# Token loads, side stores, the last chunk and the first gather moved in a one-core hybrid decoder step

## What is computed

```
mod = silu(c) @ w_ada + b_ada                     # six vectors of 1024 for each of 9 sequences
h   = rmsnorm(x, g_pre_mix) * (1 + sc_mix) + sh_mix
u, qkv, z, a, b = split(h @ w_in)
pool_out = pool_mixer(u)                          # windows of 2, 4, 8, 16
q, k, v  = silu(causal_conv(qkv)); g, beta from a, b
o = gated_delta_rule(l2norm(q), l2norm(k), v, g, beta, state_ssm)   # needs inverses of I + L
x = x + gt_mix * rmsnorm(concat(pool_out, norm(o) * silu(z)) @ w_out, g_post_mix)
h = rmsnorm(x, g_pre_ffn) * (1 + sc_ffn) + sh_ffn
top 4 of 32 experts by h @ router_w + router_b; gates = softmax of the four
f = sum over the four: gate * (((clip(up) + 1) * glu(gate_part)) @ w_down[e] + b_down[e])
x = x + gt_ffn * rmsnorm(f, g_post_ffn)
```

## Time and profile before

| | us |
|---|---|
| median of three runs | 1183.03 |
| lowest and highest | 1180.54 and 1185.24 |
| the profiled execution | 1182.28 |
| its span | 1180.2 |

### The profile page before, as it was taken

One profiled execution on the slowest core, in us unless ns is written; L12 is line 12 of the kernel. 1 busy time (PEld: TensorE's weight loads), 2 busy tenths in 40 slices (PEclk: granted clock), 3 DMA queues, 4 the chain that ended last, 5 costly groups with the idle time before them and its releaser, 6 DMA issues.

```text
span 1180.2 us, 31873 instructions
## 1 busy us (share of the span) xinstructions
PE 1017.5 (86%) x11938; PEld 482.1 (41%) x11939; DVE 399.2 (34%) x1168; ACT 173.5 (15%) x470; POOL 123.0 (10%) x321
## 2 busy tenths in 40 slices
PE   6999998987998698997699898998766899999864
PEld 4778767453333233332133243333222333333421
DVE  2146876864231132332133332332111333332313
ACT  4253233340000010000000010000000000001102
POOL 0240130101010010010000110011000000010100
PEclk9999999999999899998899999998988999999997
DMA  9998739999999999999999988999999999999996
GB/s 334 306 348 290 260 96 331 372 391 421 427 428 428 428 430 428 428 428 429 429 428 428 427 337 371 428 429 430 427 428 430 428 429 428 427 430 428 429 428 274
DMA packets 76838, 463.07 MB, mean 392 GB/s; under 512 B 11899, under 2 KB 30145, under 8 KB 52154
## 3 DMA queue, kind: packets, MB, share of 16 engines
q1 hardware_dynamic: 73469, 460.57, 95.2%
q10 hardware_dynamic: 3333, 1.99, 0.6%
HBM read 455.56 MB, written 6.98 MB: 392 GB/s over the span
## 4 chain that ended last, share of the span: by engine, by line
PE 60%; DMA 19%; DVE 10%; SPq 5%; issue 4%; DVEq 1%; ACT 0%; another core or an unknown queue 0%; ACTq 0%
PE psum L686 26%; PE psum L705 14%; DMA weights<-in_w_gu 8%; PE psum L1077 5%; DMA work<-in_w_gu 4%; PE psum L661 4%; DMA work<-in_w_down 4%; PE psum L638 2%; SPq L970 2%; PE psum L655 2%; PE psum L1030 1%; DMA weights<-in_w_ada 1%; DVE work L2500 1%; SPq L912 1%; DVE weights L2294 1%
## 5 line engine op out<-in xcount | busy, mean ns | idle before, releaser
L686 PE MATMUL psum<-weights,work 128*32 128x512 f32 x2928 | 346.0, 613 | 89.3 <-DMA weights<-in_w_gu 42.1
L686 PEld LDWEIGHTS psum<-weights,work 128*32 128x32 f32 x2928 | 92.8, 111 | 310.6 <-issue 243.5
L705 PE MATMUL psum<-weights,work 128*32 128x256 f32 x2624 | 171.4, 415 | 34.2 <-DVE work L2514 32.0
L2500 DVE STREAM_TRANSPOSE work<-psum 128x256 f32<-128x256 f32 x53 | 23.9, 450 | 416.5 <-PE psum L686 413.8
L705 PEld LDWEIGHTS psum<-weights,work 128*32 128x32 f32 x2624 | 87.7, 118 | 111.5 <-issue 63.2
L1899 ACT ACTIVATE work<-work x53 | 22.1, 417 | 494.1 <-DVE work L2504 474.7
L2524 DVE STREAM_TRANSPOSE work<-work 128x288 f32<-128x288 f32 x53 | 25.4, 478 | 199.8 <-PE psum L661 199.8
L638 PE MATMUL psum<-work 128*32 128x257 f32 (+1 forms) x1296 | 89.2, 388 | 4.1 <-ACT work L1896 4.1
L1077 PE MATMUL psum<-work,weights 128*128 128x288 f32 x320 | 81.4, 410 | 0.0
L1077 PEld LDWEIGHTS psum<-work,weights 128*128 128x128 f32 x320 | 59.7, 190 | 17.4 <-issue 1.8
L638 PEld LDWEIGHTS psum<-work 128*32 128x32 f32 (+1 forms) x1296 | 37.7, 109 | 69.0 <-issue 60.3
(11 more groups left out here) (411 smaller groups left out, 896.3 us busy)
## 6 DMA issues: line engine op xcount, KB each, us to landing
weights<-in_w_gu SPq DMA_DIRECT2D x112, 2048.0 KB, 36.1
weights<-in_w_down SPq DMA_DIRECT2D x48, 2048.0 KB, 39.5
work<-in_w_gu SPq DMA_DIRECT2D x16, 2048.0 KB, 37.2
work<-in_w_down SPq DMA_DIRECT2D x16, 2048.0 KB, 42.7
weights<-in_w_ada SPq DMA_DIRECT2D x12, 2048.0 KB, 11.9
weights<-in_w_in SPq DMA_DIRECT2D x5, 2048.0 KB, 14.1
weights<-in_w_out SPq DMA_DIRECT2D x2, 2048.0 KB, 7.8
out<-weights SPq DMA_DIRECT2D x12, 256.0 KB, 4.5
```

What stands on the lines that cost most here:

```text
L686: last = mm(bank(GB)[SLOTS * n:SLOTS * n + SLOTS, :].rearrange("p (a x) -> p a x", a=4), xTm[:, k, :], gu[:, k % 2, n], start=k == 0, stop ...
L705: last = mm(bank(YB)[SLOTS * q:SLOTS * q + SLOTS, 0:QW], hT[:, k, :], dn[:, k % 4, QW * q:QW * q + QW], start=k == 0, stop=k == KT - 1)
L2500: v.transpose(features, of_slots[0]).then_inc(s["hid_step"], 1)
```

## The change

- **Tokens first.** The two loads of `x_sb` move from ScalarE's queue to the head of SyncE's.
- **More unread products at the start.** After `stats_set` TensorE runs three wide and sixteen small products of zeros (`cT`, which VectorE now clears before it signals `stats_set`). Behind the transposes of `c` it runs two wide ones and twenty small ones in place of three wide ones. The transposes of the prompt's `xn` now follow `ada(0)` and wait for `xn` 2; those of the samples stay. At the router `keep_warm(0, 2)` becomes `keep_warm(0, 3)`, and one more follows `logit_parts(0, 6, 7)`.
- **Gates stored ahead of solved blocks.** On SyncE the wait for `modG` and the eight side stores move ahead of the wait for the solved blocks.
- **Last chunk by halves.** `add_mix(2)`, `x1_root(2)` and `normed(2)` work in two halves of 512 columns with a signal for each; the transposes wait for each half, and the store of that chunk waits for `x1` 4.
- **Sample rows by products.** `samples_back` brings the sample rows to their partitions by products with `ident`, and one copy takes the place of four (`back(1, 6)` goes). The three `rows_back` copies now come in the order samples, chunk 0, chunk 1.
- **First gather ahead of the transposed ranks.** On VectorE the gates and `gate_col` come before `rank`; on TensorE the first gather comes before the rank and gate transposes, and inside it the wait for `h2` 3 moves from the last group of rows to the second.

```diff
         for c in range(3):
-            if first and c == 2:
+            if first and c == 1:
                 pe.wait_ge(s["h2"], 3)
...
     pe.wait_ge(s["h2"], 2)
+    pe.wait_ge(s["rank_done"], 2)
+    pe.wait_ge(s["cur_set"], 2)
+    gather_by(sel_first, GC, True).then_inc(s["xg_ps"], 1)
     pe.wait_ge(s["rank_done"], 1)
...
     last.then_inc(s["router_ps"], 1)
-    pe.wait_ge(s["rank_done"], 2)
-    pe.wait_ge(s["cur_set"], 2)
-    gather_by(sel_first, GC, True).then_inc(s["xg_ps"], 1)
     pe.wait_ge(s["cum"], 4)
...
+    sp.dma_start(x_sb[:, 0:2, :], x_prompt.rearrange("a (b p) d -> p (a b) d", p=P)).then_inc(s["x_in"], 16)
+    sp.dma_start(x_sb[0:NS, 2, :], x_sample.rearrange("b t d -> (b t) d")).then_inc(s["x_in"], 16)
     for load in LOADS[:N_EARLY]:
...
     sp.dma_start(w_out_sb[1], w_out_half(1)).then_inc(s["wout_in"], 16)
-    sp.wait_ge(s["pooled"], 2)
-    sp.wait_ge(s["t0"], 2)
-    sp.dma_start(t_dram.rearrange("c h r k i j -> (c h r) (k i j)"), blk_tu[0:BLOCKS]).then_inc(s["blk"], 16)
-    t_block_loads(sp, 0)
     sp.wait_ge(s["modG"], 4)
...
                      ).then_inc(s["side_st"], 16)
+    sp.wait_ge(s["pooled"], 2)
+    sp.wait_ge(s["t0"], 2)
+    sp.dma_start(t_dram.rearrange("c h r k i j -> (c h r) (k i j)"), blk_tu[0:BLOCKS]).then_inc(s["blk"], 16)
+    t_block_loads(sp, 0)
     sp.wait_ge(s["side_st"], 128)
...
         c = CHUNKS[i]
-        sp.wait_ge(s["x1"], i + 1)
+        sp.wait_ge(s["x1"], (1, 2, 4)[i])
         if c == 2:
...
+    pe.wait_ge(s["stats_set"], 1)
+    zeros = cT.rearrange("p k q -> p (k q)")[:, 0:P]
+    for _ in range(3):
+        mm(bank(7), zeros, zeros.unsqueeze(1).to_broadcast([P, 4, P]), start=True, stop=True)
+    for _ in range(16):
+        mm(bank(7)[:, 0:NS], zeros, zeros[:, 0:NS], start=True, stop=True)
     pe.wait_ge(s["c_in"], 48)
...
-    keep_warm(7, 3)
+    keep_warm(7, 2)
+    for _ in range(20):
+        mm(bank(7)[:, 0:NS], ident, ident[:, 0:NS], start=True, stop=True)
     pe.wait_ge(s["setup_sb"], 1)
     ada(0)
+    pe.wait_ge(s["xn"], 2)
+    for k in range(KT):
+        for c in range(2):
+            at = 256 * (k % 2) + P * c
+            last = tr(bank(4 + k // 2)[:, at:at + P], xn[:, c, P * k:P * k + P], ident)
+        if k % 2:
+            last.then_inc(s["xT_ps"], 1)
     pe.wait_ge(s["rows_in"], 16 * (N_VEC + N_HIST))
...
     last.then_inc(s["setup_ps"], 1)
-
     pe.wait_ge(s["xn"], 3)
-    for k in range(KT):
-        for c in range(2):
-            at = 256 * (k % 2) + P * c
-            last = tr(bank(4 + k // 2)[:, at:at + P], xn[:, c, P * k:P * k + P], ident)
-        if k % 2:
-            last.then_inc(s["xT_ps"], 1)
     pe.wait_ge(s["setup_sb"], 4)
...
         for k in range(KT):
+            if i == 2 and k == KT // 2:
+                pe.wait_ge(s["xn2"], 4)
             out = bank(b)[:, NS * k:NS * (k + 1)] if c == 2 else bank(b + k // 4)[:, P * (k % 4):P * (k % 4) + P]
...
+    def samples_back(b):
+
+        for k in range(KT):
+            for j in range(2):
+                g = 2 * (k % 2) + j
+                last = mm(bank(b)[NS * g:NS * g + NS, 64 * (k // 2):64 * (k // 2) + 64], h2T[:, k, span(2)],
+                          ident[:, 64 * j:64 * j + 64], start=True, stop=True)
+        last.then_inc(s["h2_ps"], 1)
+
     def ranks(c):
...
     transposes_x2(1, 1)
-    keep_warm(0, 2)
+    keep_warm(0, 3)
     logit_parts(0, 6, 7)
+    keep_warm(0, 1)
     transposes_x2(2, 4)
...
     sample_logits(1)
+    pe.wait_ge(s["s_new"], 2 * H)
+    samples_back(3)
     pe.wait_ge(s["lg_sb"], 3)
-    pe.wait_ge(s["s_new"], 2 * H)
     logit_parts(2, 1, 2)
...
     last_ranks()
-    pe.wait_ge(s["h2"], 1)
-    back(1, 6)
...
     act.dma_start(ident, cc("ident")).then_inc(s["c_in"], 16)
-    act.dma_start(x_sb[:, 0:2, :], x_prompt.rearrange("a (b p) d -> p (a b) d", p=P)).then_inc(s["x_in"], 16)
-    act.dma_start(x_sb[0:NS, 2, :], x_sample.rearrange("b t d -> (b t) d")).then_inc(s["x_in"], 16)
...
         act.wait_ge(s["ssq"], count - 1)
-        junk_of = x1_junk if i == 2 else mixjunk
-        fn(junk_of[0:n, :], x_sb[0:n, c, :], ACT.Square, scale=D ** -0.5, accum_out=st[0:n, c:c + 1]
+        if i == 2:
+            own(fn(x1_junk[:, 0:512], x_sb[:, c, 0:512], ACT.Square, scale=D ** -0.5, accum_out=st[:, 10:11]))
+            own(fn(st[:, 11:12], st[:, 10:11], ACT.Identity, bias=st[:, 12:13]))
+            act.wait_ge(s["x1"], 4)
+            fn(x1_junk[:, 512:D], x_sb[:, c, 512:D], ACT.Square, scale=D ** -0.5, accum_out=st[:, c:c + 1]
+               ).then_inc(s["ssq"], 1)
+            act.wait_ge(s["ssq"], count)
+            fn(st[:, 4 + c:5 + c], st[:, c:c + 1], ACT.Sqrt, bias=st[:, 11:12]).then_inc(s["root"], 1)
+            return
+        fn(mixjunk[0:n, :], x_sb[0:n, c, :], ACT.Square, scale=D ** -0.5, accum_out=st[0:n, c:c + 1]
            ).then_inc(s["ssq"], 1)
...
             act.wait_ge(s["h2"], n - 1)
-        rows = bank(b, 2).rearrange("p (a g x) -> p g a x", a=4, g=NQ)
+        rows = None if c == 2 else bank(b, 2).rearrange("p (a g x) -> p g a x", a=4, g=NQ)
         if c == 2:
-            for q in range(NQ):
-                last = act.copy(h2s[NS * q:NS * q + NS, 0:QW].rearrange("p (a x) -> p a x", a=4), rows[0:NS, q])
+            last = act.copy(h2s[:, 0:QW], bank(b)[:, 0:QW])
         else:
...
     modulate_prompt(2, 4)
-    rows_back(0, 6, 1)
-    rows_back(2, 4, 2)
+    rows_back(1, 3, 1)
+    rows_back(0, 6, 2)
     act.wait_ge(s["gex"], 1)
     fn(exg, exg, ACT.Exp).then_inc(s["gex"], 1)
-    rows_back(1, 6, 3)
+    rows_back(2, 4, 3)
     act.wait_ge(s["s_new"], 2 * H)
...
-    own(v.memset(st[:, :], 0.0))
+    v.memset(st[:, :], 0.0)
+    own(v.memset(cT, 0.0))
     v.memset(st[:, 12:13], EPS)
...
-    own(v.memset(cT, 0.0))
     v.memset(ab, 0.0)
...
         mixed = mix_s[0:n, :] if c == 2 else bank((6, 4)[c], 2)
+        if i == 2:
+            for m in range(2):
+                of = slice(D // 2 * m, D // 2 * (m + 1))
+                own(stt(mixed[:, of], mixed[:, of], st[:, 4 + c:5 + c], gm_tok[c][:, of], ALU.mult, ALU.mult))
+                tt(x_sb[:, c, of], x_sb[:, c, of], mixed[:, of], ALU.add).then_inc(s["x1"], 1)
+            v.wait_ge(s["x1"], 4)
+            return
         own(stt(mixed, mixed, st[0:n, 4 + c:5 + c], gm_tok[c][0:n, :], ALU.mult, ALU.mult))
...
         own(rstd(st, c, c + 1, (4, 5, 7)[i], n))
+        if i == 2:
+            for m in range(2):
+                of = slice(D // 2 * m, D // 2 * (m + 1))
+                ts(xt[c][:, of], x_sb[:, c, of], st[:, 4 + c:5 + c], None, ALU.mult).then_inc(s["xn2"], 1)
+            return
         ts(xt[c][0:n, :], x_sb[0:n, c, :], st[0:n, 4 + c:5 + c], None, ALU.mult).then_inc(s["xn2"], 1)
...
     own(v.reciprocal(rst[:, 3:6], rst[:, 0:3]))
+    tt(gate, exg, rst[:, 3:6].unsqueeze(2).to_broadcast([P, 3, NE]), ALU.mult).then_inc(s["gate_done"], 1)
+    v.wait_ge(s["gate_done"], 1)
+    ts(gate_col[:, 0:2 * NQ].rearrange("p (c g) -> p c g", c=2), gate[:, 0:2, 0:1].to_broadcast([P, 2, NQ]),
+       1.0 / ALPHA, None, ALU.mult).then_inc(s["cur_set"], 1)
+    ts(gate_col[:, 2 * NQ:], gate[:, 2, 0:1], 1.0 / ALPHA, None, ALU.mult).then_inc(s["cur_set"], 1)
     v.wait_ge(s["router_ps"], 6)
...
     step = Chain(v, s["hid_step"])
-    tt(gate, exg, rst[:, 3:6].unsqueeze(2).to_broadcast([P, 3, NE]), ALU.mult).then_inc(s["gate_done"], 1)
     step(ts(cnt_i, bank(0)[:, 3 * NE:4 * NE], 1.0, float(SLOTS - 1), ALU.max, ALU.add))
...
        rank[:, :, 0:1].to_broadcast([P, 3, SLOTS]), ALU.is_equal).then_inc(s["rank_done"], 1)
-    v.wait_ge(s["gate_done"], 1)
-    ts(gate_col[:, 0:2 * NQ].rearrange("p (c g) -> p c g", c=2), gate[:, 0:2, 0:1].to_broadcast([P, 2, NQ]),
-       1.0 / ALPHA, None, ALU.mult).then_inc(s["cur_set"], 1)
-    ts(gate_col[:, 2 * NQ:], gate[:, 2, 0:1], 1.0 / ALPHA, None, ALU.mult).then_inc(s["cur_set"], 1)
```

## The result

The changed kernel is slower: 1190.84 us, median of five runs (1185.25 to 1193.35), against 1181.23 for the kernel before beside it; the ratio is 1.0060, 95% interval 1.0043 to 1.0078. The prediction was 1181.7 us, at most 1186.5. The profiled execution took 1192.73 us, with a span of 1190.6, that is 10.4 more than before. So the loss is not the same in every execution, and no trace of a short one is on record.

What follows compares the result with a forecast made beforehand. A TensorE, VectorE, transfer chain bounds the first 180 us, back-to-back expert loads the time from 234 us. 1182.28 + 1.5 (start) - 2.1 (stores) = 1181.7 us; range 1176.5 to 1186.5.

Steps and rivals of the forecast that it cites:

- the added products: Start: extra unread TensorE products delay `ada(0)` and so `ada(1)`; +1.5 us, bounds 0 to +2.5.
- The stores, forecast at -2.1: Middle: side stores first let state loads issue 6.0 us sooner; 2.1 us pass, ending the wait at `sample_reads`.
- a rival of 0.06: Start: clock stays lower through the small products, every pass doubles, `ada(0)` ends at 27 to 32; 1189 to 1194 us; chance 0.06.
- TensorE's chain from `ada(1)` to 180 us: First 180 us: TensorE, then VectorE, then transfers decide; TensorE is full behind `ada(1)` to 180 us.
- the cost of the blocks: Middle: state loads start while the second queue's block loads are in flight; 0 to +0.9 us, taken as 0.
- nothing is being fed: 160 to 180 us: DMA share 0.52; a gain there can start everything behind it sooner.
- Tokens and head at nothing: Token loads first at the start, and edits from the last chunk to the first gather: each costed at nothing.
- the 9.6 us of queued transfers: First reload, 263.28 us: about 9.6 us of older transfers lie ahead, covering shifts of expert 0's start.
- one of the prediction's own signs of being wrong: Head of the experts: the prediction is wrong if the DMA share falls below 1 between 250 and 300 us.
- the second rival: Edits miss the path: stores 0, start +1.5 to +2.5, blocks up to 0.9; 1183 to 1185.7 us; chance 0.20.
- the forecast: Whole kernel: the main case, 1179.5 to 1184 us by its bounds; chance 0.59.

Runs made afterwards that it cites:

- the start alone: Kernel before with only the new unread products at the start, and `cT` cleared ahead of `stats_set`: 1192.95 us, ratio 1.0064.
- the 128 columns: Changed kernel with its 36 small products at the start 128 columns wide in place of 32: 1183.29 us, ratio 1.0008.
- the head edits alone: Kernel before with only the edits from the last chunk on (halves, sample rows, gates, first gather ahead, keep-warm products): 1182.95 us, ratio 0.9998.
- the kernel with wide products: Changed kernel with wide unread products only at the start, five of zeros and five of `ident`, no small ones: 1184.13 us, ratio 1.0013.
- the stores alone: Kernel before with only the side stores moved ahead of the solved blocks: 1185.25 us, ratio 1.0013.
- tokens alone: Kernel before with only the two token loads moved to the head of SyncE's queue: 1181.89 us, ratio 0.9995.
- states held: Kernel before with side stores moved ahead and state loads waiting for the last use of a ring slot: 1185.95 us, ratio 1.0026.
- the start undone: Changed kernel with the first unread products of the kernel before; `xn` transposes stay behind `ada(0)`: 1184.66 us, ratio 1.0015.
- the twenty only: Changed kernel without the sixteen small products of zeros; the twenty small ones stay: 1191.24 us, ratio 1.0061.

## Why the prediction was wrong

**The term that was wrong: the added products, +1.5 us forecast, +9.6 measured.** The step that failed is the choice of the row. The small passes were priced at 0.125 us from line 1502, "of the same shape". The sixteen did take 0.125 each (3.99 us for 32), and the table shows where the rest went:

| | forecast us | measured us |
|---|---|---|
| three wide, to their end | 7.0 | 6.6 |
| sixteen small | 4.0 | 4.0 |
| transposes of `c` | 0.6 | 1.0 |
| two wide | 1.98 | 3.78 |
| twenty small | 5.0 | 8.6 |
| `ada(0)` | 1.95 | 3.5 |

Everything up to 10 us is right within 0.4 us; everything behind is at the lower clock. The stores, forecast at -2.1, brought nothing when alone (+1.5 us by the ratio), so that no second term made up for this one. The row of line 1502 was right for one pass, and three products can't show what a row of twenty does to the clock. The price of a product was taken to be its length, and its effect on what runs behind it was put into a rival of 0.06.

**That rival is what happened, in the main.** It said 0.25 us a pass (0.215 measured for the twenty), `ada(0)` ending at 27 to 32 us (26.90), and 1189 to 1194 us (1190.84). Its place is confirmed by the start alone, and that the small products are the cause by the 128 columns. Its path is not: it had the clock low from the first pass on and the sixteen at 8.0 us. They took 3.99, and the fall came during them. Nor did the 2.1 us that it took off for the stores show by themselves. That its time fits so well is in part luck. Its evidence was underrated: the prediction read from the earlier trace rows that the first products of the start run at the lower level and that the clock column can't be trusted there, and should have taken a forecast that rests on full speed in that place as no better than even. The Trainium skill, "TensorE: Matmul & The Clock Gate", Part 1, which it cited there, warns of a fall where the array idles between groups; here the rows show a fall with TensorE recorded busy 2.00 of 2.00 us, so that busy time was no evidence against it.

**TensorE's chain from `ada(1)` to 180 us carries a delay in full:** right, since 9.6 us at 39.77 are 9.6 at L574 (179.65 against 170.06).

**The stores, -2.1 us.** States directly behind the blocks, no wait at `sample_reads`: right, and so is the cost of the blocks taken at nothing (their loads land after 1.8 us in the median with the states behind them, as before). The step that failed is that TensorE's own order would stay as it was: a stall of 2.2 to 2.9 us inside that order appears in five of the seven traces with the moved stores and in none of the six others (0.74 at most). Between 160 and 180 us "nothing is being fed" (a DMA share of 0.52) was read as room; it may also be what kept TensorE undisturbed. The net is +0.13% alone, and -2.4 us in the one trace where the stall stayed away.

**Tokens and head at nothing:** right, 0.9995 and 0.9998. The cover that the head rests on varies: the first reload lands after at least 14.5 us before, 9.3 with the head edits alone, and 7.8 in the kernel with wide products, where the DMA share fell to 0.84 between 270 and 280 us. That is one of the prediction's own signs of being wrong, and it came in that run, not in the changed kernel. So the 9.6 us of queued transfers is not a fixed reserve.

**The range** ended at 1186.5 us and left out a rival whose whole price was known. Two bounds are also off by their own terms: 1182.28 + 1.5 is 1183.8, not 1183, at the lower end of the second rival, and 1182.28 - 2.1 is 1180.2, not 1179.5, at that of the forecast. Neither bears on the failure.

## What to carry to other kernels

Price an unread product by the clock it leaves behind, not by its length alone. In these traces the clock held behind products of 128 and 512 columns and fell, or stayed down, behind those of 32, which took as long as those of 128. A stretch with few transfers in it isn't free room; look for what runs undisturbed in it before moving a bulk load there. When a rival's full cost can be worked out and the view that speaks against it is one you have just called untrustworthy, give it more than a few per cent.

## What the runs showed of the hardware

- 32 passes with 128x128 float32 weights take 3.88 us at 128 columns and 3.99 at 32, so the narrow product saved nothing. 72 passes of 32 columns ended with the granted clock at 0.50; the same 72 at 128 columns with it at 1.00.
- At the lower level a pass of 32 columns took 0.215 us (8.58 for 40), against 0.125 at the upper one (3.99 for 32).
- The old start is not safe either, and the cause of that is open. In the profiles of the stores alone and of the head edits alone TensorE waits 1.43 and 1.27 us at 17.9 and 17.6 us (for `in_state_pool`), the granted clock is 0.50 from 22 to 26 us, and `ada(1)` starts at 33.0 and 32.6 us instead of 30.2. Both are at the time of before within 0.2%. After waits of 0.77 and 0.49 us at the same place (tokens alone, states held) the clock stayed at 1.00.
- The granted clock reads 1.00 in the first 8 us of the changed kernel, though its six wide passes take 5.19 us, 0.87 each, nearer the 0.92 of the earlier trace rows than the 0.50 of the earlier trace rows.
- With the eight state loads in flight directly behind the blocks, TensorE stood 2.2 to 2.9 us in the middle of a group of products, with no semaphore to wait for, in five of seven profiles, and 1.03 and 0.30 at most in the other two; with the loads held back it did not. In four of the five the granted clock then fell to 0.50, for some 3 to 13 us (0.50 from 180 to 190 us in the start undone, 1.00 in before); in the twenty only it stayed at 1.00.
